# Two-layer hybrid encoder on one core: conditioning units placed anew in the first mixer, and X turned on PE in the triangular inverse

## The reference, cut to what matters

```
for layer in range(2):
    ada = silu(c) @ ada_w[layer] + ada_b[layer]
    sh1, sc1, gt1, sh2, sc2, gt2 = jnp.split(ada, 6, axis=-1)
    h = modulate(rmsnorm(x, norm_mix_w[layer]), sh1, sc1)
    x = x + gt1 * token_mixer(h, ...)
    h = modulate(rmsnorm(x, norm_ffn_w[layer]), sh2, sc2)
    f = swiglu(h, ...) if layer == 0 else moe_swiglu(h, ...)
    x = x + gt2 * f
# in the token mixer, per head (4) and chunk of 64 tokens:
lmat = where(strict, einsum(k_beta, k) * decay, 0)
t_mat = triangular_solve(eye + lmat, eye)          # inverse of a unit lower triangle
```

## Time and profile before

| | us |
|---|---|
| median of 3 runs | 1867.36 (1862.92 to 1867.83) |
| the profiled execution, its own time | 1867.36 |
| its span in the trace | 1865.6 |
| PE busy | 1793.8 (96%) |
| DVE busy | 1497.6 (80%) |
| ACT busy | 1060.8 (57%) |

### The profile page before, as it was taken

One profiled execution on the slowest core, in us unless ns is written; L12 is line 12 of the kernel. 1 busy time (PEld: TensorE's weight loads), 2 busy tenths in 40 slices (PEclk: granted clock), 3 DMA queues, 4 the chain that ended last, 5 costly groups with the idle time before them and its releaser, 6 DMA issues.

```text
span 1865.6 us, 26157 instructions
## 1 busy us (share of the span) xinstructions
PE 1793.8 (96%) x10014; PEld 1522.4 (82%) x10014; DVE 1497.6 (80%) x1449; ACT 1060.8 (57%) x905; POOL 72.0 (4%) x133
## 2 busy tenths in 40 slices
PE   5998999899999999999999999999999999999997
PEld 5878887899997879887778888888888888888775
DVE  6778757977766766466998899888898988889898
ACT  2463233433334472255667777777777777777765
POOL 4010000000000010000000001000000000000000
PEclk8999998999999999999999999999999999999999
DMA  8635636798873514245999999999999999999994
GB/s 300 202 100 194 186 130 203 247 318 297 281 261 110 172 55 113 68 137 205 344 341 379 378 358 388 360 370 382 359 378 369 357 393 361 374 375 362 382 390 172
DMA packets 261446, 519.94 MB, mean 279 GB/s; under 512 B 12170, under 2 KB 75892, under 8 KB 261364
## 3 DMA queue, kind: packets, MB, share of 16 engines
q1 hardware_dynamic: 257988, 506.21, 76.9%
q0 software_dynamic: 3376, 12.58, 1.7%
HBM read 510.90 MB, written 7.86 MB: 278 GB/s over the span
## 4 chain that ended last, share of the span: by engine, by line
PE 79%; DVE 13%; ACT 3%; issue 2%; DMA 2%; SPq 0%; DVEq 0%; ACTq 0%
PE bank L1047 18%; PE bank L1049 18%; PE bank L1048 18%; PE bank L1053 6%; PE bank L1054 5%; PE bank L1055 5%; DVE ada_acc L1693 2%; DVE w_lo L1675 2%; DVE w_lo L1795 2%; PE bank L1609 1%; ACT w_hi L958 1%; DMA ring<-in_w_in_dram 1%; PE bank L1351 1%; DMA ring<-in_moe_w_up_dram 1%; PE bank L1068 1%
## 5 line engine op out<-in xcount | busy, mean ns | idle before, releaser
L1795 DVE TENSOR_TENSOR w_lo<-ring,w_hi 128x2048 fp32r<-128x2048 f32 x336 | 767.0, 2290 | 96.6 <-ACT w_hi L958 92.8
L958 ACT CAST w_hi<-ring 128x2048 fp32r<-128x2048 f32 x336 | 642.3, 1912 | 134.6 <-PE bank L1049 127.4
L1047 PE MATMUL bank<-w_hi,xg_hi 128*128 128x512 f32 x896 | 357.3, 399 | 0.8 <-DVE w_lo L1795 0.7
L1049 PE MATMUL bank<-w_hi,xg_lo 128*128 128x512 f32 x896 | 352.9, 394 | 0.0
L1048 PE MATMUL bank<-w_lo,xg_hi 128*128 128x512 f32 x896 | 352.9, 394 | 0.0
L1675 DVE TENSOR_TENSOR w_lo<-ring,w_hi 128x2048 fp32r<-128x2048 f32 x96 | 219.7, 2291 | 87.0 <-ACT w_hi L729 86.6
L1053 PE MATMUL bank<-hT_hi,w_hi 128*128 128x256 f32 x912 | 266.6, 292 | 10.7 <-DVE w_lo L1675 6.6
L1054 PE MATMUL bank<-hT_lo,w_hi 128*128 128x256 f32 x912 | 259.5, 284 | 0.0
L1055 PE MATMUL bank<-hT_hi,w_lo 128*128 128x256 f32 x912 | 259.4, 284 | 0.0
L729 ACT CAST w_hi<-ring 128x2048 fp32r<-128x2048 f32 x96 | 182.5, 1904 | 82.3 <-PE bank L1049 45.7
L1047 PEld LDWEIGHTS bank<-w_hi,xg_hi 128*128 128x128 f32 x896 | 168.1, 188 | 43.1 <-issue 2.7
(11 more groups left out here) (418 smaller groups left out, 2140.0 us busy)
## 6 DMA issues: line engine op xcount, KB each, us to landing
ring<-in_moe_w_gate_dram SPq DMA_DIRECT2D x112, 1024.0 KB, 7.4
ring<-in_moe_w_up_dram SPq DMA_DIRECT2D x112, 1024.0 KB, 7.5
ring<-in_moe_w_down_dram SPq DMA_DIRECT2D x112, 1024.0 KB, 7.5
ring<-in_ada_w_dram SPq DMA_DIRECT2D x48, 1024.0 KB, 5.5
ring<-in_w_in_dram SPq DMA_DIRECT2D x38, 1024.0 KB, 5.3
ring<-in_ffn_w_gate_dram SPq DMA_DIRECT2D x14, 1024.0 KB, 7.0
ring<-in_ffn_w_up_dram SPq DMA_DIRECT2D x14, 1024.0 KB, 5.1
ring<-in_ffn_w_down_dram SPq DMA_DIRECT2D x14, 1024.0 KB, 6.6
```

The lines of the kernel that those rows point to most:

```text
L958: act.copy(w_hi[MOE_BUF[p % NS_MOE]][:], ring[:, p % RING, :]).then_inc(hi_ready, 1)
L1047: pe.matmul(o, xh, wh, start=start, stop=False)
L1049: return pe.matmul(o, xl, wh, start=False, stop=stop)
L1795: dve.tensor_tensor(w_lo[b][:], ring[:, p % RING, :], f32(w_hi[b][:]), ALU.subtract).then_inc(taken, 1)
```

## The change

Three things are done.

1. The list `units`: ada units 4,0 and 4,1 go ahead of the swkv unit and 5,0 behind it, the next ones stand singly behind gate units 1 to 5, two behind gate 7, two behind wa 0, and pieces 10 and 11 of layer 0 (four units) go to the FFN, ahead of those of layer 1, which then end two steps later. The two explicit calls of `take_upto` are gone. PE's `ada_piece` calls are placed to match: none in levels 1, 3 and 5, one in levels 2 and 4, one behind each of wb 0, wb 1 and wa 1, two in the first two FFN steps.
2. The inverse: XT is not updated any more in levels 1 to 4. In levels 2 to 5 PE turns the new X into banks 2 and 3 after U's products, and ACT copies them to XT before it goes on to the next gate unit. In level 5 XT is updated as before.
3. `ada_columns` and `gate_diag` of the FFN's gate move from step 12 to step 2, layer 1's `ada_columns` behind the loop, and some small results and the gate row change banks.

```diff
+        if l == 0:
+            ada_units(2)
         units.append((("swkv", l), True))
+        if l == 0:
+            ada_units(1)
         for j in (6, 7):
             units.append((("qkvz", l, j), True))
-        if l == 0:
-            ada_units(3)
         for j in range(8):
             units.append((("gate", l, j), True))
             if l == 0:
-                ada_units((1, 1, 1, 2, 2, 0, 0, 0)[j])
+                ada_units((0, 1, 1, 1, 1, 1, 0, 2)[j])
         for cc in range(2):
             units.append((("wb", l, cc), True))
-            if l == 0:
-                ada_units(2)
         for cc in range(2):
             units.append((("wa", l, cc), True))
             if l == 0 and cc == 0:
...
-    ada1 = [("ada", 1, q, kh) for q in range(NQ) for kh in range(2)]
+    ada1 = ada0 + [("ada", 1, q, kh) for q in range(NQ) for kh in range(2)]
...
                 for j in range(6):
+                    if j > 1:
+                        for tb in range(TB):
+                            act.wait_ge(xt_ps, 8 * l + 2 * (j - 2) + tb + 1)
+                            act.copy(XT[:, tb * H:(tb + 1) * H, :],
+                                     ps[2 + tb][:].rearrange("p (h c) -> p h c", h=H)).then_inc(xt_s, 1)
                     gate(j)
...
-                    warm(24, 0)
+                    warm(24, 1)
...
                         ins.then_inc(u_ps, 1)
+                    if lev > 1:
+                        for tb in range(TB):
+                            for h in range(H):
+                                ins = pe.transpose(ps[2 + tb][:, h * P:(h + 1) * P], X[:, tb * H + h, :], ident[:])
+                            ins.then_inc(xt_ps, 1)
                     pe.wait_ge(gate_s, 8 * l + lev)
                     two_blocks(("gate", l, lev), 0)
-                    if l == 0 and lev != 2:
-                        ada_piece(0, {1: 5, 3: 6, 4: 7, 5: 8}[lev], 1)
+                    if l == 0 and lev in (2, 4):
+                        ada_piece(0, 4 + lev // 2, 1)
...
                         pe.wait_ge(u_s, 10 * l + 2 * (lev - 1) + tb + 1)
+                        if lev > 1:
+                            pe.wait_ge(xt_s, 8 * l + 2 * (lev - 2) + tb + 1)
...
                             if lev < 5:
-                                pe.matmul(ps[6 + tb][:, h * P:(h + 1) * P], XT[:, n, :], U[:, n, :],
-                                          start=True, stop=True)
-                            ins = pe.matmul(ps[2 + tb][:, h * P:(h + 1) * P], U[:, n, :], XT[:, n, :],
-                                            start=True, stop=True)
+                                ins = pe.matmul(ps[6 + tb][:, h * P:(h + 1) * P], XT[:, n, :], U[:, n, :],
+                                                start=True, stop=True)
+                            else:
+                                ins = pe.matmul(ps[2 + tb][:, h * P:(h + 1) * P], U[:, n, :], XT[:, n, :],
+                                                start=True, stop=True)
...
-                        if i < NQ:
-                            ada_piece(1, i, 3)
+                        if i < 2:
+                            ada_piece(0, NQ - 2 + i, 2)
+                        else:
+                            ada_piece(1, i - 2, 3)
...
-                    gate_row(2, f_dg, (2, 3))
+                    pe.wait_ge(fs_s, 2 * FC)
+                    gate_row(2, f_dg, (2, 0))
                     f_down(2 * FC - 1)
...
                 divide(1)
-                if l == 0:
-                    take_upto(u_of[("ada", 0, 4, 0)])
                 out_low(0)
-                if l == 0:
-                    take_upto(u_of[("ada", 0, 5, 0)])
...
-                        if lev < 5:
-                            dve.tensor_tensor(X[:, heads, :], X[:, heads, :],
-                                              ps[6 + tb][:].rearrange("p (h c) -> p h c", h=H), ALU.subtract)
-                        dve.tensor_tensor(XT[:, heads, :], XT[:, heads, :],
-                                          ps[2 + tb][:].rearrange("p (h c) -> p h c", h=H),
+                        to, bank = (X, 6 + tb) if lev < 5 else (XT, 2 + tb)
+                        dve.tensor_tensor(to[:, heads, :], to[:, heads, :],
+                                          ps[bank][:].rearrange("p (h c) -> p h c", h=H),
                                           ALU.subtract).then_inc(xx_s, 1)
...
-                    ada_columns(0, 1, NQA, NQ)
+                    ada_columns(0, 1, NQA, NQ - 2)
...
+                            ada_columns(0, 2, NQ - 2, NQ)
                             dve.wait_ge(ada_s, 3)
                             gate_diag(2, 0, 5, f_dg[:])
-                        if i == NQ:
-                            ada_columns(1, 3, 0, NQ)
...
+                    ada_columns(1, 3, 0, NQ)
+                    dve.wait_ge(ada_s, 4)
                     ahead(("fd", 2 * FC - 1), 0)
-                    gate_copy(2, f_gt, (2, 3))
+                    gate_copy(2, f_gt, (2, 0))
```

More of the change, by code:

```diff
@@ L389, in build_program @@
         xx_s = sem("x_updated")
+        xt_ps = sem("x_transposed_in_psum")
+        xt_s = sem("x_transposed_copied")
         ks_ps = sem("ks_in_psum")
@@ L1440, in _ @@
                 if l == 0:
-                    ada_piece(0, 9, 1)
+                    ada_piece(0, 7, 1)
                 half_branch("wb", 1, (0, 5), ob_hi, ob_lo, 0)
@@ L1445, in _ @@
                 if l == 0:
-                    ada_piece(0, 10, 1)
+                    ada_piece(0, 8, 1)
                 pe.wait_ge(oa_s, l + 1)
                 branch("wa", 0, (6, 7), oa_hi, oa_lo)
-                if l == 0:
-                    ada_piece(0, 11, 1)
                 half_branch("wa", 1, (4, 5), oa_hi, oa_lo, 0)
@@ L1453, in _ @@
                 half_branch("wa", 1, (4, 5), oa_hi, oa_lo, 1)
+                if l == 0:
+                    ada_piece(0, 9, 1)
                 for kh in range(2):
@@ L1499, in _ @@
                             f_down(i - 1)
-                        if i < NQ:
-                            ada_piece(1, i, 3)
+                        if i < 2:
+                            ada_piece(0, NQ - 2 + i, 2)
+                        else:
+                            ada_piece(1, i - 2, 3)
                         if i == 1:
                             pe.wait_ge(upper_s, 1)
-                            pe.matmul(ps[2][:, 0:P], ones[:], upper[:], start=True, stop=True)
-                            pe.matmul(ps[2][:, P:P + 2], upper[:], ones[:, 0:2], start=True,
+                            pe.matmul(ps[2][:, P:2 * P], ones[:], upper[:], start=True, stop=True)
+                            pe.matmul(ps[2][:, 2 * P:2 * P + 2], upper[:], ones[:, 0:2], start=True,
                                       stop=True).then_inc(logit_ps, 1)
-                    gate_row(2, f_dg, (2, 3))
+                    pe.wait_ge(fs_s, 2 * FC)
+                    gate_row(2, f_dg, (2, 0))
                     f_down(2 * FC - 1)
@@ L2080, in _ @@
                             dve.wait_ge(logit_ps, 1)
-                            dve.tensor_copy(slots[:], ps[2][:, 0:P])
+                            dve.tensor_copy(slots[:], ps[2][:, P:2 * P])
                             for tb in range(TB):
[L2083 to L2086, removed]
-                        if i == NQ:
-                            ada_columns(1, 3, 0, NQ)
+                                dve.tensor_scalar(tok_c[:, tb, 0:1], ps[2][:, 2 * P:2 * P + 1], float(tb * P), None, ALU.add)
+                            dve.tensor_scalar(spare, ps[2][:, 2 * P:2 * P + 1], float(2 * T), None, ALU.add)
+                            dve.tensor_scalar(spare_n, ps[2][:, 2 * P:2 * P + 1], -1.0, -float(2 * T), ALU.mult, ALU.add)
+                            link(dve.tensor_scalar(rsm[:, 0, :], ps[2][:, P:P + E], -1.0, float(E), ALU.mult, ALU.add))
+                            ada_columns(0, 2, NQ - 2, NQ)
                             dve.wait_ge(ada_s, 3)
                             gate_diag(2, 0, 5, f_dg[:])
+                    ada_columns(1, 3, 0, NQ)
+                    dve.wait_ge(ada_s, 4)
                     ahead(("fd", 2 * FC - 1), 0)
-                    gate_copy(2, f_gt, (2, 3))
+                    gate_copy(2, f_gt, (2, 0))
                     for tb in range(TB):
```

## The result

The changed kernel takes 1837.6 us (median; 1835.6 to 1840.51, 4 runs), the kernel before in the same session 1865.41 (1862.92 to 1867.83): ratio 0.985, 95% interval 0.984 to 0.987. It is faster by 27.8 us. The direction, the places and most of the mechanism were right; one term was taken for twice its size. The forecast also set out from 1867.4 us, where the kernel before measured 1865.41 here: 2.0 us of the 10.5 between 1848.1 and 1837.6 are in this start.

The account below looks back on a forecast made before the run. PE was taken as the bound nearly everywhere, with time to win where it waits, runs at half clock or sheds work. Terms -2.4 + 1.95 + 0.8 - 7.0 + 0.1 - 5.3 - 9.1 + 1.6 = -19.3 from 1867.4: 1848 us, range 1842 to 1858.

Parts of the forecast that it names:

- The step that failed: Inverse, per level: 16 products leave, 16 transposes come; period 11.85 to 11.25, -2.4 us in layer 1, -5.3 in layer 0.
- the scores to level 1: Layer 0's attention, without ada units on DVE until level 1's gate unit, becomes layer 1's stretch: 54.5 to 47.5, -7.0 us.
- The FFN's +1.6 for two pieces: FFN: two more ada pieces on PE at 0.81 us each, +1.6 us; the other moved work lies beside PE's products.
- the wait at swkv: Before layer 0's inverse: units 4,0 and 4,1 on DVE delay swkv's w_lo, +1.95 us, plus +0.8 for a possible clock fall.
- Gate 1's wait: Layer 0, gate 1: PE's idle 2.48 us for w_lo, with half clock behind it, was to go.
- The recurrence: Layer 0: nothing changes; units 8,0 and 8,1 (5.9 us on DVE) fall into its wait of 8.12 before wb 0.
- The branches: Layer 0, wb 0 to mix: 39.8 to 30.7, -9.1 us, including a 3.5 wait before wa 1 and one half-clock stretch.
- The spare before X's update: Inverse, per level: DVE finishes at 11.6, X's next update is due at 12.3, so 0.7 us is spare.
- 1 (clock in the inverse): Transposes in a row lower the clock: one more half-clock stretch per level, 13 us come back, 1861; chance 0.05.
- 2 (ACT's detour): Inverse: copies, cast and w_lo come 1 to 2 us later, X's update waits in eight levels, +10, 1858; chance 0.06.
- 3 (ada in the way elsewhere): Waits at swkv and wa 1 paid in full with the clock, another before wb 0: 5 to 6 us, 1854; chance 0.08.
- 4: Slower: the clock does not come back between the inverse's levels, PE's work there takes twice as long: +84, 1932; chance 0.02.

Follow-up runs that it names:

- the changed kernel's second profile: The changed kernel run once more, unaltered, to see how far times and half-clock stretches repeat: 1839.1 us (1838.1 to 1840.6, 4 runs).

## Why the prediction was wrong, and where it was right

**The step that failed** is in the inverse: "Then PE turns 16 blocks: sixteen such take 1.91 to the end of the last, 1.78 by start distance. PE's work is unchanged (16 products leave, 16 transposes come)". Two token blocks of four heads are eight blocks. The count of 16 goes by the trace's records: the prediction has "32 products from 718.20 to 721.76", where the code issues 16. (The "eight small products" of an ada piece in the description of the kernel before are four in the code, with eight records.) Sixteen was right for the products' time (16 records less, 1.78 forecast, 1.72 measured) and wrong for the transposes, which take one record each. The term is 0.80 and not 1.78, four times in each layer: with it the forecast's own sum gives a period of 10.27, and 10.35 was measured, in place of 11.25. The two stages measured 3.4 and 3.6 us below the forecast, 7.1 together. The kernel with sixteen transposes in a level measured 46.7 and 44.9 for them, against forecasts of 46.6 and 45.0. With this term right (eight times 0.98 less) the forecast would have been 1840 and its range, moved with it, 1834 to 1850, which holds the measured 1837.6.

**The other 3 us.** First, the scores to level 1 were priced by layer 1's 47.5, whose row shows a granted clock of 0.96: it holds a half-clock stretch of its own. Without one it takes 46.45, and 46.4 in layer 0, so the term was -8.0 and not -7.0. Windows of PE in the kernel before show where it is:

```profile
684.00:687.70 3.70, 3.33 (x4) 0.54 0.00 0
...
783.00:786.80 3.80, 3.80 (x19) 0.55 0.00 0
```

Second, in this profile of before three stretches at half clock (these two, and one in the FFN) stand where the changed kernel's profile has none: 1.0, 1.55 and 1.3 us. A fourth such difference, the stretch from about 35 to 46 us at half clock before and 1.00 after, is not in this sum, since PE did not get to its next wait later for it (66.48 before, 67.72 after). The FFN's +1.6 for two pieces is right (272.0 with a half-clock stretch against 270.4 with one); without the stretch it showed as +0.3. The three stretches are not the change's doing as far as the runs tell: the changed kernel's second profile has one of them again. How often each falls in each kernel was not counted, but the mean granted clock of each run shows the sum of them. Of nine runs of the kernel before in the first group, the three at 0.985 took 1866.85 to 1867.77 and the six at 0.989 to 0.992 took 1862.3 to 1865.9; the changed kernel took 1835.6 and 1836.8 at 0.996, and 1838.4 and 1840.5 at 0.994 and 0.990. The profile of before is one at 0.985, that of the changed kernel one at 0.996, which fits 30.6 between the two profiles and 27.8 between the medians.

**Right.** The place of the wait at swkv, if not its size: 2.75 us were forecast with the clock; the wait was 1.54 and the clock did not fall behind it. +3.0 came in the profiled pair, but 1.24 of it lies ahead of 67 us, before the units that moved (the first mixer's wait at 66.48 is at 67.72), and spreading the units took back 1.75. So 2.75 for 3.0 is luck. Gate 1's wait went. The recurrence hid its units. The branches came to 30.72 where 30.7 was worked out, with a wait of 3.52 for 3.5 and a half-clock stretch behind it. The spare before X's update was 0.65 for 0.7, and only 0.43 was paid for the 1.24 of a doubled copy.

**The rivals.** 1 (clock in the inverse): 1.00 in all eight levels, and also with twice the transposes. The rule that was weighed against it (the Trainium skill, TensorE: Matmul & The Clock Gate, Part 4: PE-mode transpose) says that the full clock does not engage for PE's transposes; no window here shows that, with eight or with sixteen in a row between matmuls. 2 (ACT's detour): no. 3 (ada in the way elsewhere): the two waits that it named are real, 1.5 and 3.5, and were in the sum; no third one came. 4: no.

The range was too narrow at its lower end because it moved only waits and clocks. It had no case for a wrong count of instructions.

## What to carry to other kernels

Count instructions in the code and take only the time of one from the trace: one instruction can stand there as one record or as two, and two operations with the same duration in a row need not be recorded alike. When a stage of the same kernel is the yardstick for another, look at its granted clock first, and take the disturbed stretch out of the yardstick. A late unit is best moved into a wait of the engine that prepares it: whole gaps of DVE (2.5 before swkv, 2.5 before wb 1) took a half piece each without a later start on PE, and one half piece in DVE's queue ahead of work that PE was already waiting for cost its 2.8 in full and the clock besides.

## What was not expected of the hardware

- An fp32 transpose of 128 x 128 on PE takes 0.10 us by start distance (eight in 0.80), an fp32 product of the same size 0.23 (eight in 1.84). Turning a result is less than half as dear as computing its transpose anew.
- The length of one wait of PE does not tell whether the clock falls behind it. It fell after 1.80, 2.48, 3.52 and 4.35 us and stayed at 1.00 after 1.53, 1.54 and 1.59, which looks like an order; but in the changed kernel it stayed also after 3.10 and 2.67, the second being the wait of 2.65 at 341.75 behind which it fell in the kernel before. In the kernel with the inverse alone a half-clock stretch lies behind a wait of 1.30 (0.56 in 680.05 to 683.60). The prediction's reading of the clock at swkv, between 1.59 and 2.48, had no more to rest on than two waits. PE's timeline in the changed kernel and the windows behind its two waits, then the wait of the kernel before and its window:

```profile
42.26 0.55 PE L1136 MATMUL bank<-hT_hi,w_hi 128*128 128x256 f32 x1 [3.10 <-DVE hT_lo L1745]
...
318.96 0.38 PE L1060 MATMUL bank<-hT_hi,w_hi 128*128 128x256 f32 x1 [2.67 <-DVE w_lo L1693]
```

```profile
42.30:45.80 3.50, 3.50 (x16) 1.00 0.75 260
319.00:322.50 3.50, 3.50 (x29) 1.00 1.03 384
```

```profile
341.75 0.39 PE L1053 MATMUL bank<-hT_hi,w_hi 128*128 128x256 f32 x1 [2.65 <-DVE w_lo L1675]
...
342.50:346.00 3.50, 3.50 (x19) 0.54 1.04 364
```

- One stretch at half clock cost 0.84 to 1.55 us, and which of them appear differs between two executions of one program, while undisturbed stages repeat to within 0.04 us.
